# Stick-breaking attention: remainders on VectorE, rounded exponentials on ScalarE

## The reference

```
z = (q k^T) / 8, for 128 queries at a time and all keys up to them
mask = query > key
log_beta = log_sigmoid(z)
log_1m = where(mask, log_sigmoid(-z), 0)
suffix = reverse cumulative sum of log_1m over the keys, less log_1m
a = exp(where(mask, log_beta + suffix, -inf))
o = a v
```

## Time and profile before

| | us |
|---|---|
| median of 3 runs | 3273.29 |
| lowest and highest | 3272.98, 3275.23 |
| the profiled execution, its own time | 3275.83 |
| its span, first to last instruction | 3274.5 |
| TensorE busy in the span | 3066.6 (94%) |
| VectorE busy | 2060.0 (63%) |
| ScalarE busy | 1026.8 (31%) |
| GpSimd busy | 1016.5 (31%) |
| mean granted TensorE clock | 0.983 of full speed |

### The profile page before, as it was taken

The page is one execution under the profiler, slowest core; times in us unless marked ns, Lnnn a source line. Parts: engine busy times, 40 slices in busy tenths (PEclk is TensorE's granted clock), DMA queues, the critical chain, the costliest instruction groups (busy, mean ns, idle before and its releaser), DMA issues.

```text
span 3274.5 us, 39112 instructions
## 1 busy us (share of the span) xinstructions
PE 3066.6 (94%) x15672; PEld 2493.8 (76%) x15672; DVE 2060.0 (63%) x3036; ACT 1026.8 (31%) x1791; POOL 1016.5 (31%) x760
## 2 busy tenths in 40 slices
PE   8999989999999999999899899999999988889988
PEld 5977767888478888879676677488888976777767
DVE  4756876555665554574578555656757676677576
ACT  3135773000231111132257400322233125521363
POOL 2004776453210000001068677300002035541153
PEclk9999999999999999999999999999999999999989
DMA  7501003333321212114101355332222220023200
GB/s 241 166 23 30 11 30 103 110 105 112 122 78 55 74 52 77 52 54 158 52 1 40 93 162 168 133 120 103 103 77 65 91 81 27 14 78 103 81 1 26
DMA packets 206931, 267.79 MB, mean 82 GB/s; under 512 B 29360, under 2 KB 133760, under 8 KB 206112
## 3 DMA queue, kind: packets, MB, share of 16 engines
q1 hardware_dynamic: 204672, 265.30, 25.2%
q10 hardware_dynamic: 2080, 0.01, 0.0%
HBM read 254.65 MB, written 10.52 MB: 81 GB/s over the span
## 4 chain that ended last, share of the span: by engine, by line
PE 36%; DVE 7%; POOL 2%; ACT 2%; issue 2%; DMA 1%; SPq 0%; DVEq 0%; POOLq 0%; ACTq 0%
PE ps L380 14%; PE ps L2089 5%; PE ps L2099 5%; PE ps L2603 2%; PE ps L1392 2%; PE ps L1375 1%; PE ps L733 1%; PE ps L1345 1%; PE ps L3023 1%; PE ps L1157 1%; DVE stat L675 1%; POOL p_lo L3280 0%; DVE w_lo L412 0%; DMA U<-w_o_dram 0%; PE ps L1332 0%
## 5 line engine op out<-in xcount | busy, mean ns | idle before, releaser
L775 POOL TENSOR_TENSOR ht_lo<-HT,ht_hi 128x1024 fp32r<-128x1024 f32 x28 | 69.9, 2500 | 964.0 <-DVE X L728 577.2
L2089 PE MATMUL ps<-ht_hi,w_hi 128*128 128x512 f32 (+1 forms) x832 | 285.5, 343 | 12.5 <-POOL ht_lo L775 10.5
L2089 PE MATMUL ps<-ht_lo,w_hi 128*128 128x512 f32 (+1 forms) x832 | 284.2, 342 | 0.0
L2089 PE MATMUL ps<-ht_hi,w_lo 128*128 128x512 f32 (+1 forms) x832 | 284.1, 341 | 0.0
L2099 PE MATMUL ps<-w_hi,a_hi 128*128 128x512 f32 x640 | 251.1, 392 | 4.3 <-DVE a_lo L2224 4.3
L2099 PE MATMUL ps<-w_lo,a_hi 128*128 128x512 f32 x640 | 250.1, 391 | 0.0
L2099 PE MATMUL ps<-w_hi,a_lo 128*128 128x512 f32 x640 | 249.9, 390 | 0.0
L380 PE MATMUL ps<-w_lo,ht_hi 128*128 128x320 f32 (+2 forms) x800 | 244.6, 306 | 0.0
L613 DVE SCALAR_TENSOR_TENSOR U<-U,stat 128x512 f32<-128x512 f32 x224 | 220.8, 986 | 13.0 <-DMA U<-w_ada_dram 3.2
L1560 POOL TENSOR_TENSOR p_lo<-ring,p_hi 128x512 fp32r<-128x512 f32 x156 | 200.4, 1297 | 87.2 <-DVE p_hi L1515 65.0
L380 PE MATMUL ps<-gate_ht_hi,gate_w_hi 128*128 128x512 f32 (+1 forms) x576 | 212.1, 368 | 11.6 <-POOL w_lo L1742 6.4
(11 more groups left out here) (453 smaller groups left out, 8284.6 us busy)
## 6 DMA issues: line engine op xcount, KB each, us to landing
ring<-w_dram SPq DMA_DIRECT2D x30, 2048.0 KB, 7.8
U<-w_ada_dram SPq DMA_DIRECT2D x80, 512.0 KB, 3.7
ring<-w_in_dram SPq DMA_DIRECT2D x48, 512.0 KB, 6.5
ring<-w_in_dram SPq DMA_DIRECT2D x8, 1280.0 KB, 6.1
ring<-a_w_in_dram SPq DMA_DIRECT2D x8, 1280.0 KB, 6.6
U<-w_ada_dram SPq DMA_DIRECT2D x4, 2048.0 KB, 15.1
hi_scratch<-ht_hi SPq DMA_DIRECT2D x2, 3072.0 KB, 9.0
gate_ht_hi<-hi_scratch SPq DMA_DIRECT2D x8, 768.0 KB, 4.4
```

The lines of the kernel that those rows point to most:

```text
L775: pool.tensor_tensor(HT_LO[:, :, tokens], HT[:, :, tokens], HT_HI[:, :, tokens].bitcast(F32), ALU.subtract).then_inc(ht_ready.sem, 1)
L2089: last = pe.matmul(ps[:, g % 4, 0:c1 - c0], lhsT, rhs, start=(k + j == 0), stop=(k == KD - 1 and j == 2))
```

## The change

VectorE makes the remainder sp_lo in all units, right behind the rounding copy sp_hi, and GpSimd makes none. ScalarE makes the rounding copy e_hi of a unit, right behind the exponentials and waiting for them, and VectorE makes none. GpSimd keeps e_lo and y_lo. The semaphores are renamed to match: TensorE's exponents wait for one count, sp_split, that VectorE raises for every unit. Nothing else moves, and no transfer is touched.

```diff
--- before.py
+++ after.py
@@ -3347,8 +3347,7 @@
         EH = [rounded_view(f"e_hi{i}", "U", 25600 + i * 2 * S, 2, S) for i in range(EB)]
         VSH = [[rounded_view(f"vs_hi{p}{i}", "HT", (8 + 2 * p + i) * S, XT, P) for i in range(2)] for p in range(2)]
         VSL = [[rounded_view(f"vs_lo{p}{i}", "U", at + i * S, XT, P) for i in range(2)] for p, at in enumerate((7168, 10240))]
-        log_ready, sp_cast, sp_split, sp_long, ex_ready = [
-            signal(n) for n in ("log_ready", "sp_cast", "sp_split", "sp_long", "ex_ready")]
+        log_ready, sp_split, ex_ready = [signal(n) for n in ("log_ready", "sp_split", "ex_ready")]
 
         Stick = namedtuple("Stick", "block at")
 
@@ -3365,8 +3364,7 @@
             BANKS = 3
             PAIRS = SB_H // 2
             LAST = PAIRS * UP
-            st_0, lg_0, sc_0, ss_0, ex_0 = st_ready.n, log_ready.n, sp_cast.n, sp_split.n, ex_ready.n
-            sl_0 = sp_long.n
+            st_0, lg_0, ss_0, ex_0 = st_ready.n, log_ready.n, sp_split.n, ex_ready.n
             p_0, pc_0, psp_0, pv_0, o_0, v_0 = p_ready.n, p_cast.n, p_split.n, pv_done.n, o_taken.n, v_split.n
             ot = OT2[1]
             out.ready.update({pair: y_split.n + pair + 1 for pair in range(PAIRS)})
@@ -3376,12 +3374,6 @@
 
             def bank(u):
                 return 2 * (u % BANKS)
-
-            def on_dve(u):
-
-                return u % UP == UP - 1
-
-            long_ones = list(itertools.accumulate([0] + [int(on_dve(u)) for u in range(LAST)]))
 
             with block(False) as b:
                 @b.tensor
@@ -3412,10 +3404,7 @@
                     def exponents(u):
                         if u >= LAST:
                             return
-                        if on_dve(u):
-                            pe.wait_ge(sp_long.sem, sl_0 + long_ones[u + 1])
-                        else:
-                            pe.wait_ge(sp_split.sem, ss_0 + u + 1 - long_ones[u + 1])
+                        pe.wait_ge(sp_split.sem, ss_0 + u + 1)
                         first = u // UP * UP
                         for sp in (SPH, SPL):
                             for h in range(2):
@@ -3475,7 +3464,10 @@
                     def exponentials(u):
                         act.wait_ge(ex_ready.sem, ex_0 + u + 1)
                         past(act, pv_done, pv_0, u + 1 - EB)
-                        act.activation(EF[u % EB][:, :, 0:size(u)], ps[:, bank(u):bank(u) + 2, 0:size(u)], ACT.Exp).then_inc(p_ready.sem, 1)
+                        e = EF[u % EB][:, :, 0:size(u)]
+                        act.activation(e, ps[:, bank(u):bank(u) + 2, 0:size(u)], ACT.Exp).then_inc(p_ready.sem, 1)
+                        act.wait_ge(p_ready.sem, p_0 + u + 1)
+                        act.activation(EH[u % EB][:, :, 0:size(u)], e, ACT.Copy).then_inc(p_cast.sem, 1)
 
                     act.preload_act_table_set("natural_log_exp_and_others")
                     logs(0)
@@ -3495,16 +3487,9 @@
                         dve_chain.link(dve, dve.scalar_tensor_tensor(a, ps[:, bank(u):bank(u) + 2, 0:size(u)], 0.0, a,
                                                                      ALU.max, ALU.add))
                         hi = SPH[u % SPB][:, :, 0:size(u)]
-                        if on_dve(u):
-                            dve_chain.link(dve, dve.tensor_copy(hi, a))
-                            dve.tensor_tensor(SPL[u % SPB][:, :, 0:size(u)], a, hi.bitcast(F32),
-                                              ALU.subtract).then_inc(sp_long.sem, 1)
-                        else:
-                            dve.tensor_copy(hi, a).then_inc(sp_cast.sem, 1)
-
-                    def rounded(u):
-                        dve.wait_ge(p_ready.sem, p_0 + u + 1)
-                        dve.tensor_copy(EH[u % EB][:, :, 0:size(u)], EF[u % EB][:, :, 0:size(u)]).then_inc(p_cast.sem, 1)
+                        dve_chain.link(dve, dve.tensor_copy(hi, a))
+                        dve.tensor_tensor(SPL[u % SPB][:, :, 0:size(u)], a, hi.bitcast(F32),
+                                          ALU.subtract).then_inc(sp_split.sem, 1)
 
                     def pair_values(pair):
                         if pair >= PAIRS:
@@ -3535,7 +3520,6 @@
                     softplus(1)
                     pair_values(0)
                     for g in range(LAST):
-                        rounded(g)
                         softplus(g + 2)
                         if g % UP == 1 and g > UP:
                             output(g // UP - 1)
@@ -3546,14 +3530,6 @@
 
                 @b.gpsimd
                 def _(pool):
-                    def softplus_rest(u):
-                        if u >= LAST or on_dve(u):
-                            return
-                        n = size(u)
-                        pool.wait_ge(sp_cast.sem, sc_0 + u + 1 - long_ones[u])
-                        pool.tensor_tensor(SPL[u % SPB][:, :, 0:n], SPF[u % SPB][:, :, 0:n],
-                                           SPH[u % SPB][:, :, 0:n].bitcast(F32), ALU.subtract).then_inc(sp_split.sem, 1)
-
                     def rest(u):
                         n = size(u)
                         pool.wait_ge(p_cast.sem, pc_0 + u + 1)
@@ -3565,20 +3541,14 @@
                         pool.tensor_tensor(Y2L[1][:, pair, :], ot[:, pair, :], Y2H[1][:, pair, :].bitcast(F32),
                                            ALU.subtract).then_inc(y_split.sem, 1)
 
-                    softplus_rest(0)
-                    softplus_rest(1)
                     for g in range(LAST):
                         rest(g)
-                        softplus_rest(g + 2)
                         if g % UP == 2 and g > UP:
                             output_rest(g // UP - 1)
                     output_rest(PAIRS - 1)
                     pool.wait_ge(y_split.sem, y_split.n + PAIRS)
-            for sg in (st_ready, log_ready, ex_ready, p_ready, p_cast, p_split, pv_done):
+            for sg in (st_ready, log_ready, ex_ready, sp_split, p_ready, p_cast, p_split, pv_done):
                 sg.n += LAST
-            for sg in (sp_cast, sp_split):
-                sg.n += LAST - long_ones[LAST]
-            sp_long.n += long_ones[LAST]
             for sg in (o_taken, v_split, y_cast, y_split):
                 sg.n += PAIRS
             out.finish(range(3, KD), lambda pe: pe.wait_ge(o_taken.sem, o_0 + PAIRS))
```

## The result

The change makes the kernel slower: 3287.14 us, median of 10 runs (3283.26 to 3294.09), against 3276.22 us of the kernel before in the same comparison (3272.98 to 3282.70). The ratio is 1.0035 with an interval of 1.0027 to 1.0043, or +11.5 us (+8.8 to +14.1). The forecast was +4.2 us, called the same, and the range ended at 3283.5; the sign was right, the size was not. The profiled execution of the changed kernel, whose rows follow, took 3293.91 us, 6.8 above that median; 4.3 us of its difference from the profile before lie ahead of the stage.

What follows compares the result with a forecast made beforehand. TensorE, busy 94% of the span, bounds the kernel; in the stage it waits for GpSimd results. Start and pairs 0, end +2.7, clock +1.5 sum to +4.2 us: median 3273.29 to 3277.5 us, called the same, range 3270.5 to 3283.5.

Steps and rivals of the forecast that it cites:

- Step 4: In each pair, GpSimd's e_lo of the next pair's second unit goes ahead of VectorE's 1024-column sp_lo remainder: 1.69 us.
- The start: First pair: first unit's remainder 1.0 us sooner, third unit's 1.5 later, net +0.5; with the pairs' -0.9, taken as 0.
- The end: After the last unit: its copy and e_lo delay the first output product, 5.13 us behind the Exp, not 2.41: +2.7 us.
- The clock: Behind TensorE's 4.1 us idle before the first output product, 3 us at half speed: +1.5 us, bounds 0 and 3.
- The wait for e_lo of u2: TensorE's 1.97 us wait ahead of the value products of a pair's third unit (1024 columns) would go.
- rival A: Slower: e_lo of a pair's first unit also gets ahead of the second unit's remainder: 3281.3 to 3285 us, chance 0.25.
- the loop itself: The steady pair, from the third unit's exponents to the next pair's, takes 16.88 us against 17.06: 0.2 us less.
- steps 3 and 4: In each pair, VectorE's softplus sum and cast take 1.99 us, then GpSimd's e_lo precedes VectorE's 1024-column remainder: 1.69 us.
- rival C: Faster: both TensorE waits of each pair, 2.9 us together, simply go, and the start gains 1.0: 3262.0 us, chance 0.05.

Runs made afterwards that it cites:

- e4: The changed kernel with the last unit's e_hi copy made by VectorE again: 3282.91 us, ratio 1.0023 to the kernel before.
- e0: The changed kernel run again without any edit: ratio 1.0038 to the kernel before, +12.4 us.
- e8: e2 with seven TensorE products on zeros ahead of the second unit's exponents in pairs 1 to 5: ratio 1.0014 to the kernel before, +4.6 us.
- e9: The changed kernel with nine TensorE products on zeros ahead of the second unit's exponents in pairs 1 to 5: ratio 1.0026 to the kernel before, +8.5 us.
- e10: The changed kernel with the last copy on VectorE, the value split one unit earlier and nine zero products together: ratio 0.9999 to the kernel before, -0.3 us.
- e3: The changed kernel with VectorE's split of the next pair's values one unit earlier: ratio 1.0013 to the kernel before, +4.3 us.
- e1: The changed kernel with the e_hi casts back on VectorE, so only the sp_lo remainders move: ratio 0.9987 to the kernel before, -4.3 us.
- e2: The kernel before with only the e_hi copies moved to ScalarE, GpSimd keeping its 12 remainders: ratio 1.0056, +18.3 us.

## Why the prediction was wrong

**What held.** The prices were right: the copies take 0.85 and 1.06 us, the 768-column remainder 0.96, and e_lo starts 0.08 us behind a copy's end. Step 4 was right where the pair ran in the predicted order: u2's remainder took 2.72 and 2.73. The start gave back 0.9 us of the predicted 1.0. The end was right almost to the row: 5.15 us from the Exp to the first output product (5.13 predicted), idle 4.14 (4.1), the clock at half behind it. The clock took 2.0 us there rather than 1.5, and in e4's profile all of it goes with that copy. The wait for e_lo of u2 went as predicted, and in the second pair a wait ahead of u2's exponents (1.58 us) took its place.

**The step that failed first: "The clock."** It was a part of its own, and it looked at one idle only, the one at the end. The pairs were summed at full clock without a word on why they would keep it: a term put at nothing without a reason. It measured 10.6 us of TensorE's busy time in the stretch, 3.4 of them up to the second pair's u1 and 7.2 behind; in e0's profile 9.6, of which 0.7 and 8.9. In the profiled execution the forecast for the stretch was +2.7 (the end's idle, the pairs at nothing) and it became +12.7; idle time was 0.6 under the forecast, so by size the clock is the whole error. How much of it a single execution pays is in part luck: of two idles of 3.48 us one kept the clock. That half clock and not a slower operand or another contention makes such a loss is shown by e8, with more work for TensorE and less time. For the changed kernel itself e9's profile says the same (busy time 94.87 with 45 products more, against 95.02), its times don't prove it alone; e10 shows that fillers, the early split and the last copy on VectorE together undo the loss. The rows that should have warned were in rows 10: half clock behind 3.47 us, full clock behind 2.83 us, and rival A would have made an idle near that in every pair. A was priced by its wait alone, at 3281.3 to 3285; with what the clock adds it might have reached the measured time. The kernel before had its 2.9 us in two pieces, of 1.97 and 0.93. From its third pair on, the change joins its idle time into one of 2.4 to 3.5.

**The second step: the loop itself, steps 3 and 4.** They gave 16.88 us a pair and assumed that one fixed order repeats. The idle time came out near the forecast, but from the third pair on in the wrong place and in one piece, and where the clock is kept the pairs are too long by this alone: e9's stretch, at 0.96, is 6.3 us over before, 3.6 more than the end's idle. At full clock the pair lasts 17.7 when the value split is caught (0.8 over the forecast, 0.6 over before) and 16.8 in e3, where it isn't. The failing thought was that VectorE's load is unchanged and so its queue is: I followed which engine holds the port at u2's and u1's remainders, but not at the value split, which stands between them. Rival A did occur, and the value split was worse than A, 3.48 us of idle against 2.6. As rival A's own text had it, these losses exclude each other in part: 1.23 us for u2's remainder in every pair where another was caught.

**The halves.** e1 and e2 split the change cleanly: the remainders are a gain (-4.3 us), the copies a loss (+18.3), and together they give +11.5, less than the copies alone. Why less isn't shown; GpSimd has less to do in the change (44.06 against 62.59 us in the stretch). Only the first half was worth making. The rule of the Trainium skill behind rival C ("GPSIMD Engine Reference", Engine selection) spoke of where the arithmetic belongs, and e1 bears it out for the remainders (-4.3 us); as the prediction had said, a price is not a place on the path.

**What stays open.** What the clock goes by is not settled. It fell behind idles of 1.58 (in the second pair of the change, from 3161.70), 1.81, 2.62 and 3.48 us and held behind 1.58 (in e0, at 3155.95), 1.97, 2.61, 3.48 (in the change, at 3190.63) and 3.51 (in e0, at 3228.05). Nor is it known why the time at half clock at the start of the stretch is 6, 8 or 16 us. e2 idles less in its stretch than the kernel before (15.3 against 16.7 us) at a much lower clock, so the sum of idle time does not decide either. e9's time above its profile is not explained either; it is about the size by which other sums differ from their runs.

## What to carry to other kernels

A cast that sits on a busy engine also sets when the engine behind it may start: before moving it, list every operation that its consumer will now run beside, the small ones too, and see whether the waits that are left fall together. Judge waits of TensorE also by whether the engine stays at full clock behind them: one wait of two or three us can cost several more at half speed, and a few products on zeros in its place took 12 us off e2. And split such a change into its halves at once: here one half was a gain hidden under the other.

## What the runs showed of the hardware

- TensorE fell to the 1.2 GHz level behind an idle of only 1.81 us, in every steady pair of e2, and stayed there for over 8 us while fully busy (0.50 from 3184.69 to 3193.00). Of two idles of 2.61 and 2.62 us in one execution of e0, one was followed by 10 us at 0.50 and the other by full clock; so it was with two of 3.48 us in the changed kernel.
- The same kernel ran its first exponents at half clock for 16 us in one execution and for 6 in another.
- 35 extra products on zeros made e2 some 12 us faster by the medians (3291.90 to 3279.75, the kernel before at 3275.95 and 3276.03).
- The port changes hands in turn: e_lo (2.40 us), then the waiting vs_lo, then y_lo (1.50), then the waiting vs_hi. A 256-column operation of 0.43 us took 2.66, six times its own length, so what this collision cost went by the other engine's instruction, not by VectorE's own.
- Fewer collisions did not mean less time: VectorE is busy 64.80 us in the stretch of e2 (+18.3 us) and 76.23 in that of e8 (+4.6), with the same instructions.
